# Even mixer: conditioning steps between the halves of a level and none in the last two, masks and differences reordered, rotary part by pairs of heads

## What is computed

```python
def gla_chunked(q, k, v, log_g, s0, include_diag):   # one direction
    ...
        b = jnp.cumsum(gi.astype(jnp.float32), axis=-2)
        diff = b[:, :, :, None, :] - b[:, :, None, :, :]
        decay = jnp.exp(jnp.where(mask[:, :, None], diff, -jnp.inf)).astype(qi.dtype)
        att = jnp.einsum('bhid,bhjd,bhijd->bhij', qi, ki, decay)
        o_intra = jnp.einsum('bhij,bhjv->bhiv', att, vi)
        o_inter = jnp.einsum('bhid,bhdv->bhiv', qi * jnp.exp(b).astype(qi.dtype), s)
    ...
def apply_rope(x, cos, sin):
    x0, x1 = x2[..., 0], x2[..., 1]
    out = jnp.stack([x0 * cos - x1 * sin, x0 * sin + x1 * cos], axis=-1)
    ...
        s = jnp.einsum('bqhd,bkhd->bhqk', qi, k).astype(jnp.float32) * scale
        p = jax.nn.softmax(s, axis=-1).astype(v.dtype)
        return jnp.einsum('bhqk,bkhd->bqhd', p, v)
```

## Time and profile before

| | us |
|---|---|
| runs | 3288.84 median (3288.74 to 3291.86) |
| profiled execution: time, span | 3291.22, 3289.4 |
| TensorE matmuls busy | 3038.2 (92%) |
| VectorE, ScalarE, GpSimd busy | 1379.4, 1072.6, 242.4 |
| levels, first pairs to start of cq | 1733.6 to 1826.9 |
| score 0 of the latent attention | 1923.3 |
| mean granted TensorE clock | 0.953 |

### The profile page before, as it was taken

One profiled execution on the slowest core, in us unless ns is written; L12 is line 12 of the kernel. 1 busy time (PEld: TensorE's weight loads), 2 busy tenths in 40 slices (PEclk: granted clock), 3 DMA queues, 4 the chain that ended last, 5 costly groups with the idle time before them and its releaser, 6 DMA issues.

```text
span 3289.4 us, 45808 instructions
## 1 busy us (share of the span) xinstructions
PE 3038.2 (92%) x19910; PEld 2353.2 (72%) x19910; DVE 1379.4 (42%) x2098; ACT 1072.6 (33%) x1580; POOL 242.4 (7%) x275
## 2 busy tenths in 40 slices
PE   6988899779999989999897888999999999898998
PEld 4866699755555547888676646888868887774898
DVE  4655554432222234333477354333343333436554
ACT  4433354222222223222342233322242222435443
POOL 0014470110000000000004000000000000200000
PEclk9988899979999999999999899999989999998999
DMA  7457754389999953232249221333222323310453
GB/s 229 155 181 229 247 157 138 107 320 389 391 393 392 391 232 112 81 115 69 79 137 307 88 77 52 99 93 104 77 88 90 103 88 102 131 65 1 141 182 101
DMA packets 415222, 537.41 MB, mean 163 GB/s; under 512 B 14340, under 2 KB 389924, under 8 KB 390308
## 3 DMA queue, kind: packets, MB, share of 16 engines
q1 hardware_dynamic: 415012, 534.38, 47.7%
HBM read 533.30 MB, written 1.05 MB: 162 GB/s over the span
## 4 chain that ended last, share of the span: by engine, by line
PE 82%; DVE 8%; ACT 5%; DMA 3%; issue 2%; SPq 0%; POOL 0%; DVEq 0%; ACTq 0%; POOLq 0%
PE ps L189 79%; PE ps L188 2%; DVE ar L244 2%; ACT ar L314 2%; DMA RAW<-in_ada_w 1%; DVE LR L244 1%; ACT HR L314 1%; DMA RAW<-in_w_in 1%; DVE ar L260 1%; DVE ar L250 1%; PE ps L195 1%; ACT arf1i L314 1%; DVE ar L263 1%; ACT L314 1%; DVE ar L254 1%
## 5 line engine op out<-in xcount | busy, mean ns | idle before, releaser
L189 PE MATMUL ps<-AH,HR 128*128 128x512 f32 (+1 forms) x2552 | 897.1, 352 | 45.6 <-DVE AL L244 18.4
L189 PE MATMUL ps<-AL,HR 128*128 128x512 f32 (+1 forms) x2552 | 888.4, 348 | 0.0
L189 PE MATMUL ps<-AH,LR 128*128 128x512 f32 (+1 forms) x2552 | 887.6, 348 | 0.0
L244 DVE TENSOR_TENSOR LR<-RAW,HR 128x2048 fp32r<-128x2048 f32 (+3 forms) x232 | 485.9, 2096 | 598.9 <-ACT HR L314 594.8
L314 ACT ACTIVATE HR<-RAW 128x2048 fp32r<-128x2048 f32 (+3 forms) x232 | 404.3, 1744 | 726.5 <-PE ps L189 628.5
L189 PEld LDWEIGHTS ps<-AH,HR 128*128 128x128 f32 x2552 | 492.4, 193 | 117.2 <-ACT AH L314 14.3
L189 PEld LDWEIGHTS ps<-AH,LR 128*128 128x128 f32 x2552 | 492.3, 193 | 59.0
L189 PEld LDWEIGHTS ps<-AL,HR 128*128 128x128 f32 x2552 | 492.8, 193 | 57.1
L189 PE MATMUL ps<-ar 64*128 64x128 f32 (+9 forms) x1318 | 238.6, 373 | 36.4 <-DVE ar L244 18.8
L244 POOL TENSOR_TENSOR ar<-ar 128x384 f32<-128x384 f32 (+5 forms) x138 | 153.0, 1117 | 1308.1 <-DMA ar<-in_cst 1024.0
L189 PEld LDWEIGHTS ps<-ar 64*128 64x128 f32 (+2 forms) x1318 | 140.4, 188 | 117.4 <-issue 46.6
(11 more groups left out here) (187 smaller groups left out, 3566.9 us busy)
## 6 DMA issues: line engine op xcount, KB each, us to landing
RAW<-in_ada_w SPq DMA_DIRECT2D x72, 1024.0 KB, 6.6
RAW<-in_f1i SPq DMA_DIRECT2D x44, 1024.0 KB, 5.1
RAW<-in_f2i SPq DMA_DIRECT2D x44, 1024.0 KB, 5.1
RAW<-in_w_in SPq DMA_DIRECT2D x32, 1024.0 KB, 5.7
RAW<-in_w_ada SPq DMA_DIRECT2D x24, 1024.0 KB, 8.2
RAW<-in_w_eu SPq DMA_DIRECT2D x17, 1024.0 KB, 9.9
HF<-in_w_ed SPq DMA_DIRECT2D x17, 1024.0 KB, 8.9
LF<-in_w_eu SPq DMA_DIRECT2D x17, 1024.0 KB, 10.1
```

The costliest lines, as they stand in the source:

```text
L189: return self.e.matmul(o, w, x, start=start, stop=stop)
L244: return self.e.tensor_tensor(o, a, b, op) if self.e else NOTHING
```

## The change

- `level_steps(n)` is 1 for levels 0 to 11 and 0 for 12 and 13. TensorE runs one step between the halves of a level and one behind it; ScalarE and VectorE run both behind their work of the level. Levels 12 and 13 have none, so steps 7 to 30 lie in the levels.
- On VectorE `referred` (difference) and `weighted` (product) are separate. `referred(0)` goes ahead of the diagonal's products, `referred(n + 1)` stays ahead of the masks of level n, `weighted(n + 1)` stands between the masks of its two halves. One wait for VectorE's own last mask stands ahead of the four masks instead of one ahead of each.
- The rotary pieces are three: the key (256 columns), heads 0 and 1 and heads 2 and 3 (512 columns each). Score n waits for its own pair of heads. The third piece follows the maximum of score 0 on VectorE.
- Steps 31 to 33 stand between the rotary matmuls and the loop (on VectorE behind the third piece), steps 34 to 36 in n = 0 to 2. The four splits of `oT` are spread over n = 0 to 3.

```diff
-        self.xs = [self.qr[Q, i, 256:512] for i in range(4)] + [self.krr[Q, 256:512]]
+        self.xs = [self.krr[Q, 256:512].unsqueeze(1)] + [self.qr[Q, i:i + 2, 256:512] for i in (0, 2)]
...
+def level_steps(n):
+
+    return 1 if n < 12 else 0
...
-    def pairs(n, k, q):
+    def pairs(n, k, q, steps=0):
 
         for tp in range(2):
+            T.step(steps if tp else 0)
...
     for n, (lv, d) in enumerate(o.levels):
         T.wait_ge(*dve.of("kq", n))
         T.wait_ge(*pool.of("kq", n))
-        pairs(n, o.KQ[n % 2], o.KQ[n % 2])
-        T.step(2)
+        pairs(n, o.KQ[n % 2], o.KQ[n % 2], level_steps(n))
+        T.step(level_steps(n))
...
     for n in range(14):
         if n < 13:
             referred(n + 1)
-        S.step(2)
+        S.step(2 * level_steps(n))
...
+    def referred(n):
+        lv, d = o.levels[n]
+        w = 1 << lv
+        bv, dv = (o.halves(x, w) for x in (o.bs[d], o.KQ[n % 2]))
+        ref = (bv[:, :, 0, w - 1:w] if d == 0 else bv[:, :, 1, 0:1]).broadcast_to([128, 512 // w, w])
+        lo = bv[:, :, 0, :]
+        V.wait_ge(*pe.of("att", n - 2 if n > 1 else -1, 1, 1))
+        if d == 0:
+            V.tt(dv[:, :, 0, :], ref, lo, SUB).then_inc(*dve("referred", n))
+        else:
+            V.tt(dv[:, :, 0, :], lo, ref, SUB).then_inc(*dve("referred", n))
+
+    def weighted(n):
+        lv, d = o.levels[n]
+        w = 1 << lv
+        dv, kv, qv = (o.halves(x, w) for x in (o.KQ[n % 2], o.kT, o.qT))
+        V.wait_ge(*act.of("kq", n))
+        V.tt(dv[:, :, 0, :], dv[:, :, 0, :], (kv if d == 0 else qv)[:, :, 0, :], MUL).then_inc(*dve("kq", n))
+
+    referred(0)
     V.wait_ge(K.loaded["glam"], 16)
     for tp in range(2):
...
-        V.wait_ge(*act.of("kq", n))
-        V.tt(dv[:, :, 0, :], dv[:, :, 0, :], (kv if d == 0 else qv)[:, :, 0, :], MUL).then_inc(*dve("kq", n))
-
-    referred(0)
+    weighted(0)
     for n, (lv, d) in enumerate(o.levels):
         if n < 13:
             referred(n + 1)
+        V.wait_ge(*dve.of("att"))
         mk = o.glam[:, 7 * d + lv:7 * d + lv + 1, :].bitcast(U32).broadcast_to([128, 4, 128])
         for tp in range(2):
             for p in range(2):
                 V.wait_ge(*pe.of("att", n, p, tp))
-                V.wait_ge(*dve.last)
                 V.put(o.ATT[p][tp], mk, K.ps("att", n, p, tp)[:, :].rearrange("p (a b) -> p a b",
                                                                              a=4)).then_inc(*dve("att"))
                 K.free(dve, "att", n, p, tp)
-        V.step(2)
+            if n < 13 and tp == 0:
+                weighted(n + 1)
+        V.step(2 * level_steps(n))
...
     for i, x in enumerate(o.xs):
-        T.mm(bank("turned rope", i)[Q, 0:256], o.rsw[Q, :], x, True, True).then_inc(*pe("rope", i))
-    T.wait_ge(*dve.of("rope"))
+        c = 256 * x.shape[1]
+        T.mm(bank("turned rope", i)[Q, 0:c].rearrange("p (a b) -> p a b", b=256), o.rsw[Q, :], x, True,
+             True).then_inc(*pe("rope", i))
+    T.step(3)
     for n in range(19):
         if n < 16:
             hd, qt, nk = o.work[n]
+            T.wait_ge(*dve.of("rope", 1 + hd // 2))
             s = slice(qt * 128, qt * 128 + 128)
...
+    S.step(3)
...
-            S.wait_ge(*dve.of("rope"))
             S.wait_ge(*dve.of("mmax", n))
...
-    for i, x in enumerate(o.xs):
+
+    def rope(i):
+
+        x, c = o.xs[i], o.xs[i].shape[1]
+        t = o.P[2][Q, 0:256 * c].rearrange("p (a b) -> p a b", b=256)
+        cos, sin = (y[Q].unsqueeze(1).broadcast_to([64, c, 256]) for y in (o.cos, o.sin))
         V.wait_ge(*pe.of("rope", i))
-        V.tt(x, x, o.cos[Q], MUL).then_inc(*dve())
-        then(V.tt(o.P[0][Q, 0:256], K.ps("turned rope", i)[Q, 0:256], o.sin[Q], MUL))
+        V.tt(x, x, cos, MUL).then_inc(*dve())
+        then(V.tt(t, K.ps("turned rope", i)[Q, 0:256 * c].rearrange("p (a b) -> p a b", b=256), sin, MUL))
         K.free(dve, "turned rope", i)
-        then(V.tt(x, x, o.P[0][Q, 0:256], ADD), "rope")
+        then(V.tt(x, x, t, ADD), "rope", i)
+
+    rope(0)
+    rope(1)
...
-    for m in range(4):
-        split(m, o.oT[:, m, :])
     for n in range(19):
         if n < 16:
             i, nk = n % 3, o.work[n][2]
@@ -2939,7 +2962,12 @@
             V.wait_ge(*pe.of("msc", n))
             then(V.red(mx, K.ps("msc", n)[:, 0:nk], MAX))
             then(V.ts(mx, mx, -(192.0 ** -0.5), None, MUL), "mmax", n)
+        if n == 0:
+            rope(2)
+            V.step(3)
         V.step()
+        if n < 4:
+            split(n, o.oT[:, n, :])
         if n >= 3 and n % 4 == 2:
```

## The result

The changed kernel takes 3302.51 us (median of 6 runs, 3296.81 to 3305.1) beside 3288.79 of the kernel before (6 runs, 3285.02 to 3291.86): ratio 1.0037, 95% interval 1.0024 to 1.0050. On another occasion it took 3298.15 beside 3288.89, ratio 1.0030 (1.0018 to 1.0042). It is slower by 0.3 to 0.4%; the forecast was 3289, its own range 3285 to 3293, and the whole, with the rivals, ended at 3296. The forecast failed.

The account below looks back on a forecast made before the run. Transfers of `ada_w` tiles at 349 GB/s were taken to bound the levels. 10.0 us lost in the latent part less 9.5 gained gave +0.5, hence 3289; own range 3285 to 3293, whole 3281 to 3296.

Parts of the forecast that it names:

- Levels: Levels 0 to 11 still take two tiles each, 6.0 us, whatever the order; four tiles fewer gain 12.0 us.
- The first rival: In the levels: evenly spaced reads lift transfers to 391 GB/s, 7.7 us faster, time 3281 to 3282; chance 0.12.
- Start: Start of the levels: exponential and pairs(0) 1.0 us earlier, tile stream restarted earlier, 2.4 us gained.
- Stall at the end of the levels: The wait for the `ewi` tile moves into level 11 ahead of cq, giving back 4.9 us.
- Rotary part worth nothing by itself: Ahead of score 0: three steps cover the shorter rotary part, score 0 at 1923.3 as before, nothing gained.
- Two cuts ahead of share 0: Start of the attention loop: cuts of `ewo0` and `ewo1` stand ahead of share 0, 8.8 us lost.
- The second rival: At the loop's start the stall on `ewo0` bites less, 4.8 us lost, time 3284; chance 0.18.
- the last term of the latent part: In the attention loop behind the late share 0: TensorE, idle for 6 us, starts slow, 1.2 us lost.
- the third: Pauses in level 11 and the latent loop each lower the clock: gain 5.7, loss 12, time 3295; chance 0.15.

Follow-up runs that it names:

- e5: Kernel before with only the new order of the levels, all 28 steps in the levels, latent part of before: 3286.72 us, ratio 0.9994.
- e2: Kernel before with the latent part of the change alone, all 28 steps staying in the levels: 3296.16 us, ratio 1.0016.
- e9: e6 with the rotary part by pairs of heads and the splits spread, loop steps still at n = 0 and 1: 3282.46 us, ratio 0.9967.
- e3: Whole change, with the two cuts of `ewo` tiles moved to rounds n = 8 and 12: 3298.61 us, ratio 1.0024.
- e4: Whole change with 5, 5 and 6 filler matmuls in TensorE's pauses at n = 0, 1, 2: 3298.36 us, ratio 1.0018.
- e10: Kernel before with six unused maxima on VectorE ahead of share 0, making it late: 3300.65 us, ratio 1.0027.
- e7: Whole change with three filler matmuls ahead of the step of n = 1 and three behind that of n = 2: 3292.92 us, ratio 1.0009.
- e1: Kernel before with the level part of the change alone, the four displaced steps falling into n = 0 to 5: 3296.51 us, ratio 1.0016.
- e11: e6 measured again, unaltered: 3278.28 us, ratio 0.9959 against the kernel before.
- e13: e1 with five filler matmuls in TensorE's rotary pause: 3289.64 us, ratio 1.0006 against the kernel before.
- e12: e6 with five filler matmuls in TensorE's rotary pause: 3287.38 us, ratio 0.9998 against the kernel before.
- again: Second profile of the changed kernel, run once more with nothing altered: 3298.15 us, ratio 1.0030 against the kernel before.
- e6: Kernel before with the changed level order and three level steps moved into TensorE's pauses ahead of the levels, 25 left there: 3282.92 us, ratio 0.9978.

## Why the prediction failed

- **Levels: right.** 5.97 us apart at 349 GB/s, the order worth nothing there and 2.6 us at the start (e5; 2.4 forecast). The `ewi` tile landed 14.0 us earlier against pairs(0); 14.4 were forecast. The first rival (391 GB/s) fell: over 1767 to 1779 us every profile shows 348 or 349. The share of 358 GB/s on the Trainium skill's page "DMA: Bandwidth & Descriptors" (section "Where 436 GB/s comes from") stays the nearest rule. The smaller term under *Start*, exponential and pairs(0) 1.0 us earlier, came to 0.6 us (pairs(0) starts 7.6 us behind pairs(-1) instead of 8.2): GpSimd's difference, now beside VectorE's, took 1.45 us instead of 1.04, and VectorE's product is last behind four diagonal products.
- **Stall at the end of the levels: right.** Cq started 11.2 us behind the landing, forecast 11.5, and at the upper clock, as forecast. Score 0 came 9.0 us earlier in the span, forecast 9.5.
- **Rotary part worth nothing by itself: right** in e2 and, on its own, in e9.
- **Two cuts ahead of share 0: right in mechanism and size.** Score 0 to `mpt` 0 is 9.6 us longer, forecast 8.8; share 0 ended at 1934.27, on the time of before. e3 shows the cuts as the cause. The second rival, a stall that bites less, fell with this.
- **The step that failed** is the last term of the latent part: "TensorE, idle for 6 us, starts slow: +1.2 us". The term names no row; I priced the lower clock as one slow start of a few matmuls, as in the earlier trace rows, where a long run of large matmuls follows. In the loop it was low for 17 us and once more at the end. The trace of before already had a low stretch of 10 us in this loop, behind the rotary pause, and I did not read it. Between `mpt` 0 and the output projection 9.9 us were lost, 8.9 of them the clock by e4, instead of 1.2. The other 1.0 is more than the sum had room for: 10.0 is 8.8 + 1.2, which leaves nothing for the splits in VectorE's chain. With 9.9 in place of 1.2 the sum is 10.0 - 1.2 + 9.9 - 9.5 = +9.2 us; the profile shows +11.2 and the two medians +13.7 and +9.3. The idle time itself was also not one pause of 6 us but four of 0.6 to 2.9.
- **The rival that held, by half,** is the third, slower by the clock: its mechanism was named, and its chance of 0.15 was too small for what I knew. Its first half failed: behind the pause in level 11 cq ran at the upper clock, and the gain was 9 to 10 us and not 5.7. Its second half, the loop, held and was too small: the loss stood at 12 us, and 19.5 were measured. "Short dependent pieces run there instead of cq" was the sentence to cost, not to mention.

The page "TensorE: Matmul & The Clock Gate" of the Trainium skill (section "HAM oscillation — how this bites in real kernels") says that waits between groups of matmuls send TensorE back to its lower clock, so that the next group starts cold. e10 and the granted clock in it agree for the fall. That the clock then stays low for 17 us (change) or 27 us (e2) of a nearly always busy TensorE is shown by the rows above, and goes beyond that example.

What stays open: why the low stretch lasts 10 us in one execution and 27 in another of the same kernel, and why it began without a pause of more than 0.8 us in e3 and e7. Because of the first the lengths of the loop in single profiles (e1, e2, e9, e11) carry some 6 us of chance; the ratios don't. How much four displaced steps cost at the upper clock throughout was therefore not reached either: e13 kept a low stretch.

## What to carry to other kernels

Price a new wait of TensorE in a loop of small dependent matmuls by the clock behind it as well: 4.3 us of waiting cost 9 here, and a few useless matmuls in the pause won 5 to 7 back. Work that is moved off a stage bound by transfers should go where both TensorE and the DMA rest (three steps there and the new order won 7 to 13 us by the ratios), not into a latency-bound loop; and what stands behind it in the queues, here the cuts that an engine makes when it takes a tile, moves with it. Filling one pause can uncover the next (e12), so look at the wait that the lower clock was hiding.

## What was not expected of the hardware

- TensorE stayed at 1.2 GHz for 17 us (change, busy in 15.67; again, busy in 15.85) and 27 us (e2, busy in 24.95; e11, busy in 22.15), and the rounds from `mpt` 0 on ran at 2.4 GHz in e4, in before, and in e7 up to its last rounds.
- In e3 and e7 the clock fell with no pause of TensorE longer than 0.77 us just ahead.
- The length of a low stretch at one place varies between executions of the same kernel, 10 and 27 us (e6, e11), and this may be part of the kernel's own scatter: 32 runs of the kernel before ranged from 3286.41 to 3298.48, its mean granted clock 0.953 in the fastest and 0.948 in the slowest. Of e11's five runs the profiled one was the slowest, 3284.64 us at 0.952, and the median one had 3278.28 at 0.955.
- GpSimd's first difference over 512 columns took 1.04 us in before, beside products of VectorE that read PSUM, and 1.45 in the change, where VectorE's own difference ran beside its start.
